# Order of small scan steps and large gate products in a woven stage: one run of products a round in place of two

## The reference

```python
h = rmsnorm(x, norm_gain)
proj = h @ w_in
(gdn_qkv, ..., nsa_z, merge) = jnp.split(proj, IN_OFFSETS, axis=-1)
ys = (gated_deltanet(...), spatial_gating(...),
      rwkv7_time_mix(...), native_sparse_attention(...))
gates = jnp.split(jax.nn.sigmoid(merge), N_MIXERS, axis=-1)
mixed = gates[0] * (ys[0] @ w_branch[0])
for i in range(1, N_MIXERS):
    mixed = mixed + gates[i] * (ys[i] @ w_branch[i])
return x + mixed @ w_out
```

## Time and profile before

| | before |
|---|---|
| median of 3 runs | 3996.52 us (3995.16 to 4002.13) |
| the profiled execution's own time | 4001.09 us |
| its span, first to last instruction | 3999.3 us |
| mean granted clock of TensorE | 0.965 of full speed |
| TensorE busy | 3767.1 us, 94% |
| VectorE, ScalarE, GpSimd busy | 2630.4, 1338.8, 1192.6 us |
| HBM traffic | 281.00 MB read, 101.22 MB written |

### The profile page before, as it was taken

The page is one execution under the profiler, slowest core; times in us unless marked ns, Lnnn a source line. Parts: engine busy times, 40 slices in busy tenths (PEclk is TensorE's granted clock), DMA queues, the critical chain, the costliest instruction groups (busy, mean ns, idle before and its releaser), DMA issues.

```text
span 3999.3 us, 51657 instructions
## 1 busy us (share of the span) xinstructions
PE 3767.1 (94%) x20718; PEld 2950.8 (74%) x20718; DVE 2630.4 (66%) x2914; ACT 1338.8 (33%) x1748; POOL 1192.6 (30%) x578
## 2 busy tenths in 40 slices
PE   8999899999879999999999998999999999998998
PEld 7567788877666666778887776888677767776777
DVE  6964887889874554378878988741455464547783
ACT  5243432234333333243323434211233232324522
POOL 2012044445313333213444441222222212221064
PEclk9999999999989999999999998999899899999999
DMA  3002223345320010222324523322312222332163
GB/s 115 21 22 90 100 100 108 108 144 195 120 80 32 32 37 22 84 106 95 101 97 166 179 97 127 106 95 95 124 62 80 68 87 73 118 94 91 39 207 139
DMA packets 131768, 385.57 MB, mean 96 GB/s; under 512 B 13564, under 2 KB 14208, under 8 KB 126280
## 3 DMA queue, kind: packets, MB, share of 16 engines
q1 hardware_dynamic: 131528, 382.27, 27.7%
HBM read 281.00 MB, written 101.22 MB: 96 GB/s over the span
## 4 chain that ended last, share of the span: by engine, by line
PE 70%; DVE 23%; ACT 4%; issue 1%; POOL 1%; DMA 1%; DVEq 0%; SPq 0%; ACTq 0%; POOLq 0%
PE ps L380 22%; PE ps L1453 22%; PE ps L476 8%; PE ps L4462 2%; PE ps L907 2%; PE ps L2250 1%; DVE xop L1626 1%; PE ps L2971 1%; DVE acc L1722 1%; PE ps L2242 1%; DVE top L1626 1%; DVE x L661 1%; PE ps L2988 1%; PE ps L3064 1%; DVE t L641 1%
## 5 line engine op out<-in xcount | busy, mean ns | idle before, releaser
L333 POOL TENSOR_TENSOR wlo<-wraw,whi 128x1024 fp32r<-128x1024 f32 x181 | 448.1, 2476 | 1700.5 <-ACT whi L325 1677.8
L1453 PE MATMUL ps<-xop,whi 128*128 128x512 f32 x1984 | 619.3, 394 | 14.6 <-DVE acc L1747 9.6
L325 ACT ACTIVATE whi<-wraw 128x1024 fp32r<-128x1024 f32 x185 | 196.1, 1060 | 899.6 <-PE ps L380 606.2
L1453 PE MATMUL ps<-top,whi 128*128 128x512 f32 x1488 | 471.3, 398 | 18.0 <-DVE acc L1716 15.0
L1453 PEld LDWEIGHTS ps<-xop,whi 128*128 128x128 f32 x1984 | 374.0, 189 | 100.0 <-DVE acc L1747 12.1
L1453 PE MATMUL ps<-xop,wlo 128*128 128x512 f32 x992 | 388.9, 392 | 0.0
L476 PE MATMUL ps<-xhalf,whi 128*128 128x512 f32 x1024 | 370.3, 444 | 0.3 <-POOL wlo L333 0.3
L1453 PEld LDWEIGHTS ps<-top,whi 128*128 128x128 f32 x1488 | 282.6, 191 | 86.2 <-DVE acc L1716 18.0
L1851 POOL TENSOR_TENSOR wlo<-wsum,whi 128x1024 fp32r<-128x1024 f32 (+2 forms) x102 | 228.7, 2242 | 363.7 <-ACT whi L1478 363.3
L380 PE MATMUL ps<-xhi,whi 128*128 128x512 f32 x868 | 307.0, 435 | 19.8 <-DVE xlo L681 8.2
L1453 PE MATMUL ps<-top,wlo 128*128 128x512 f32 x744 | 295.0, 396 | 0.0
(11 more groups left out here) (639 smaller groups left out, 7068.5 us busy)
## 6 DMA issues: line engine op xcount, KB each, us to landing
wraw<-in_w_dram SPq DMA_DIRECT2D x185, 512.0 KB, 3.7
h_keep<-h SPq DMA_DIRECT2D x154, 256.0 KB, 4.6
wraw<-in_s_dram SPq DMA_DIRECT2D x48, 512.0 KB, 4.1
f<-h_keep SPq DMA_DIRECT2D x24, 768.0 KB, 5.4
wmore<-in_s_dram SPq DMA_DIRECT2D x32, 512.0 KB, 3.9
x_keep<-x SPq DMA_DIRECT2D x16, 1024.0 KB, 3.9
g_keep<-gates SPq DMA_DIRECT2D x64, 256.0 KB, 2.4
gb<-g_keep SPq DMA_DIRECT2D x32, 512.0 KB, 4.3
```

Of the source, the lines that this page charges most:

```text
L325: se.own().activation(K.hi(c), K.raw[:, c % NRAW, :], ACT.Copy).then_inc(*K.S(("hi", c)))
L333: ge.own().tensor_tensor(K.lo(c), K.raw[:, c % NRAW, :], K.hi(c).bitcast(F32), SUB).then_inc(*K.G(("lo", c)))
L1453: d = pe.e.matmul(out[:, s, :], w[:, o], x[:, i, :], start=(j < 3 and i == 0 and t == 0), stop=(i == k - 1 and t == 2), skip_group_check=True)
```

## The change

`weave_beside` gets an argument `behind`. Where it is given, the gate products due after a step are counted up and issued only behind a step of the stream with that number, or when no stream or only the last is left. All five engines' programs call it with `behind=0`, so that the products of two steps stand together behind the delta rule's (later the sparse attention's) step, and the step of spatial gating or RWKV stands directly ahead of the next such step. `attend_streams` calls it without the argument.

```diff
-def weave_beside(gates, *streams, more={}):
-
-    live, steps = list(streams), 0
+def weave_beside(gates, *streams, more={}, behind=None):
+
+    live, steps, due = list(streams), 0, 0
     while live:
         for s in list(live):
             if next(s, StopIteration) is StopIteration:
                 live.remove(s)
             steps += 1
-            for _ in range(1 + more.get(steps, 0)):
-                next(gates, None)
+            due += 1 + more.get(steps, 0)
+            if behind is None or not live or s is live[behind]:
+                for _ in range(due):
+                    next(gates, None)
+                due = 0
...
     weave_beside(gates, in_turn(gdn_tensor(pe, K, QA, H, g), nsa_tensor(pe, K, QA, H, R.nsa)),
-                 in_turn(spatials(lambda j: spatial_tensor(pe, K, QB, H, s, j)), wait_steps(RWKV_LATER), rwkv_tensor(pe, K, QB, H, w)), more=MORE_GATES)
+                 in_turn(spatials(lambda j: spatial_tensor(pe, K, QB, H, s, j)), wait_steps(RWKV_LATER), rwkv_tensor(pe, K, QB, H, w)), more=MORE_GATES, behind=0)
```

More of the change, by code:

```diff
@@ L4351, in scans_vector @@
     weave_beside(gates, in_turn(gdn_vector(ve, K, H, g), nsa_vector(ve, K, H, R.nsa)),
-                 in_turn(spatials(lambda j: spatial_vector(ve, K, H, s, j)), wait_steps(RWKV_LATER), rwkv_vector(ve, K, H, w)), more=MORE_GATES)
+                 in_turn(spatials(lambda j: spatial_vector(ve, K, H, s, j)), wait_steps(RWKV_LATER), rwkv_vector(ve, K, H, w)), more=MORE_GATES, behind=0)
     ve.reach("scanned")
@@ L4366, in scans_scalar @@
     weave_beside(gates, in_turn(gdn_scalar(se, K, H, g), nsa_scalar(se, K, H, R.nsa)),
-                 in_turn(spatials(lambda j: spatial_scalar(se, K, H, s, j)), wait_steps(RWKV_LATER), rwkv_scalar(se, K, H, w)), more=MORE_GATES)
+                 in_turn(spatials(lambda j: spatial_scalar(se, K, H, s, j)), wait_steps(RWKV_LATER), rwkv_scalar(se, K, H, w)), more=MORE_GATES, behind=0)
     se.reach("scanned")
@@ L4376, in scans_gpsimd @@
     weave_beside(gates, in_turn(gdn_gpsimd(ge, K, H, g), wait_steps(NSA_STEPS)),
-                 in_turn(spatials(lambda j: spatial_gpsimd(ge, K, H, s, j)), wait_steps(RWKV_LATER), rwkv_gpsimd(ge, K, H, w)), more=MORE_GATES)
+                 in_turn(spatials(lambda j: spatial_gpsimd(ge, K, H, s, j)), wait_steps(RWKV_LATER), rwkv_gpsimd(ge, K, H, w)), more=MORE_GATES, behind=0)
     ge.reach("scanned")
@@ L4395, in scans_sync @@
     weave_beside(gates, in_turn(gdn_sync(sy, K, g, lambda: nsa_load(sy, K, B)), nsa_sync(sy, K, B)),
-                 in_turn(rounds(spatials(lambda j: spatial_sync(sy, K, s, j)), rwkv_first()), wait_steps(RWKV_LATER), rwkv_sync(sy, K, w)), more=LOADS_AHEAD)
+                 in_turn(rounds(spatials(lambda j: spatial_sync(sy, K, s, j)), rwkv_first()), wait_steps(RWKV_LATER), rwkv_sync(sy, K, w)), more=LOADS_AHEAD, behind=0)
     def first():
```

## The result

The changed kernel takes 4005.6 us (median of 14 runs, 4001.28 to 4013.92), the kernel before, in runs on the same chip, 3999.11 us (14 runs, 3988.82 to 4011.84). The ratio is 1.002, with a 95% interval of 1.0012 to 1.0028: slower by 0.2%, small but clear of noise. The forecast was 11 us less. The profiled execution of the changed kernel took 4011.59 us, 6 over its median, that of the kernel before 4001.09, 2 over; so the two profiles lie further apart (10.5 us of span) than the medians (6.5).

What follows compares the result with a forecast made beforehand. TensorE was taken as the bound, beside idle time and clock. Merges 13.0 us, less 2.4 for new neighbours and 1.6 for waits, plus 2.5 and minus 0.5 for slack: 11 us less, 3985.5 us, range 3969 to 4006.

Steps and rivals of the forecast that it cites:

- The number of merges: In the woven scans, runs of gate products on TensorE fall from 282 to 164, as 118 gaps go.
- The price of a merge: Each removed gap on TensorE saves about 0.11 us; 13.0 us over 118 gaps.
- The tiling rule: Changing tiling mode drains TensorE, product or not, so 41 gaps ahead of 64x64 inverse steps save only 4.5 us.
- the one on slack: VectorE's order shifts slack: waits for R's lists shrink 2.5 us, the delta rule's grow 0.5 of a possible 8.2.
- 1.6 by shorter runs: Shorter product runs lengthen TensorE's waits for VectorE, at 0.11 us for about 15 rounds, returning 1.6 us.
- The delta rule's lost slack is used up: Rival: the delta rule's waits for VectorE take the whole 8.2 us, giving 3993.5; chance 0.10.
- The clock falls more often: Rival: paired small steps on TensorE lower the clock, time at 1.2 GHz growing by half, giving 4008.5; chance 0.13.
- What would show it wrong: Signs: L3239, L3258 or L3228 above 2 us a wait, pairs growing 0.1 each, stretch clock below 0.92 or above 0.96.

Runs made afterwards that it cites:

- e9: The changed kernel, but in the second half of the delta rule's preparations the merged products stand behind R's step; 3992.32 us, ratio 0.9979 to the kernel before.
- e3: The changed kernel, but with the merged products behind the R step throughout (`behind=1`); 4010.68 us, ratio 1.003 to the kernel before.
- e6: The changed kernel, but with products behind each step again in the first half of the delta rule's preparations; 4011.49 us, ratio 1.0038 to the kernel before.
- e5: The changed kernel, but with products behind each step again in the second half of the delta rule's preparations; 3990.2 us, ratio 0.9986 to the kernel before.
- e8: e5, with products also behind each step in the sparse attention's rounds (143 to 165); 3991.03 us, ratio 0.9977 to the kernel before.

## Why the prediction was wrong, point by point

**The number of merges: right.** 282 and 164 runs were counted and are in the two traces.

**The price of a merge: right.** 0.11 us was the term for a gap, 0.11 us is measured a pair in the undisturbed stretch, the 64x64 entry stays as taken, and the stretch is shortened about as forecast (0.66 us for 24, thus 1.9 for 70, where 2 to 3 was said). This part alone is 118 x 0.11 = 13 us.

**The tiling rule: agrees as far as it goes.** The Trainium skill, "TensorEngine Tiling (Array Packing)", "Key Properties", says that a change of tiling mode drains the engine. L3592 to L2971 directly costs 0.42 us where L3592 to a product costs 0.24, so the change of tiles is paid in the direct neighbourhood as well.

**The step that failed is the one on slack**: "I take 2.5 gained and 0.5 lost, because two products or more follow most D steps, and L3239's longest wait was 1.9 us." The mechanism had been named a few sentences earlier, a product less for D behind VectorE's R list, and bounded at 8.2 us; its size was then taken near nothing. L3221, L3228 and L3239 alone went from 5.2 to 13.5 us. That these are 8.3 and the bound was 8.2 is chance: the bound was over five lines, without L3221, and those five (L3239, L3258, L3228, L3263, L2932) went from 10.7 to 14.2, since L3258, L3263 and L2932 fell. The argument looked at what follows a D step. What counts is the distance from the R step that starts VectorE's list to the D step that needs its end, and there the product was gone. The other half, the 2.5 us to be gained for R, did not come: L3659 went from 6.3 to 8.1 and L3669 from 8.6 to 10.5. All named waits together grew by 14.9 us, where the sum had them 3.6 shorter (1.6 by shorter runs, 2.0 by moved slack).

**The second term that failed is the clock**, which the sum put at nothing and left to a rival of 0.13. It fell, from 0.94 to 0.92 in the stage. Up to the first L4089 the clock records have 105.8 us at 1.2 GHz before and 129.7 after, a loss of 12 us. The account of the two profiles is then -13 for merges, +15 waits, +12 clock: +14, against +10.4 at the end of the stage. The terms overlap (a wait is longer in a slow stretch), so they are not exact. Its cause stays open. The rival had it fall by bunching; e9 and e3 have as many bunched pairs and 0.94, and the 6.2 us block ran at full clock in six kernels. It is not the length of the waits alone either: matmuls at half speed stand right behind a wait at 3002.78, but e6 waits 2.7 us less than the changed kernel and loses 10 us more to the clock. Shown is that putting the products apart (e5) or turning the pair round (e9) in the second half of D's preparations brings waits and clock back together.

**The rivals.** "The delta rule's lost slack is used up" had the right mechanism and the wrong total (3993.5), since it left the clock out. "The clock falls more often" came nearest (4008.5): it was to decide once time at 1.2 GHz grew by 22 us, and it grew by 27 in the stretch; its reason, bunching, is not borne out. The measured 4005.6 is in the range of 3969 to 4006, by 0.4 us, and on the other side of the kernel before: that it lies inside is luck, since the part of the range above 4000 was there for rivals.

**What would show it wrong** was in part well chosen: L3239, L3258 or L3228 above 2 us a wait (2.8 for L3239). But L3258 already had a wait of 2.2 us before the change, and L3221, from 0.2 to 2.6 us in all, was not on the list.

## What to carry to other kernels

When filler work is moved in front of one step to merge with other filler, look at each step that loses the filler directly ahead of it and ask what it waits for then, and which step started the work that it waits for; the total between two steps of a stream says nothing about that. Merge where the trace shows TensorE without waits, leave the filler where it covers a latency, and read the granted clock beside the waits: here its fall cost about as much as the longer waits, and no run shows what lowered it. Here the same idea, kept out of 23 rounds or turned round in them, gives 0.1 to 0.2% (e5, e9) instead of costing 0.2%.

## What the runs showed of the hardware that was not expected

A small 64x64 group directly behind a 128-wide one costs 0.18 us more than a product there (0.42 against 0.24). A block of 6.20 us of small matmuls, none of them with 512 columns over full rows, kept the full clock in six kernels and ran at 1.2 GHz for 11.43 us in one; waits of 1.83 and 1.83 us ahead of it (e6) left the clock at full, waits of 1.86 and 1.83 us (the changed kernel) had it fallen. And the kernel before varies by 23 us from run to run (3988.82 to 4011.84), as much as all effects here, and the variation goes with the clock: beside e8 and e9 its fastest run, 3990.33 us, had a mean granted clock of 0.970, and the slowest, 4013.11, one of 0.962. Single runs could not have told the kernels apart.
